# One expert item's rows fetched by a gather, and attention's preparation issued one part earlier, in a one-core decoder layer

## The chip, the core and the metric

The kernel runs on one core of a Trainium2 chip. A core has TensorE (PE, with its weight loads PEld), VectorE (DVE), ScalarE (ACT), GpSimd (POOL) and SyncE (SP), which issues transfers; they run their own instruction lists and meet at semaphores. The metric is the device time of one execution in microseconds.

## What is computed

One layer of a hybrid decoder for 512 prompt tokens and 8 x 8 sample tokens (576 rows of 1024) that share all weights, in float32. In short, from the reference:

```
u -> one projection w_in -> q_lora, kv_lora, k_rope, z, xBC, dt, gate_a, gate_b
branch A: causal conv, chunked SSD scan, gate, RMS norm -> w_branch_a
branch B: latent attention (8 heads; prompt causal, samples over 4096 cached rows) -> w_branch_b
h = LayerNorm(a*u + (sig(gate_a)*y_a + sig(gate_b)*y_b) @ w_out)
logits = h @ router_w + router_b; the top 4 of 32 experts, softmax over the 4
each expert block: rows h[row_tok], SwiGLU with clamps, scaled by the row's gate, added to y
y = LayerNorm(a*h + y)
```

The latent rows, the rotated keys and the scan's states are outputs too.

## The kernel before, in words

`program` runs a row of blocks: latents, prompt attention, sample attention, merge of branch B, convolution, scan, merge of branch A, `stage_choose` (routing), `stage_experts_combine` (experts and last norm). Each block has an instruction list per engine, written out by hand, and ends in a barrier of all engines. Most float32 operands of matmuls are split into a high and a low part (`fp32r`), and three products are summed. A plain float32 product counts as two matmul instructions in the trace, a transpose or an `fp32r` product as one.

**Prompt attention** (`stage_prompt_attention`, lines 368 to 622). 32 steps, i = 4h + q: head h, query block q of 128 rows, against keys 0 to 128(q+1). PE's step i is: the five score products of step i (lines 485 to 489), the transposes of step i-2's probabilities (496), the value products of step i-3 (505), and one of four parts of the preparation of head h+1: part 0 makes the head's query (447), part 1 its key (451), part 2 transposes its rotated query (456), part 3 the samples' query (459). ACT copies each part out with rounding (`prep_copy`, 518 to 527), and DVE forms the remainders of parts 0 to 2 (`prep_rest`, 582 to 587). Buffers of a head are used in pairs (h % 2). PE's scores of a head wait for all three remainders: `prep_low >= 3*h + 3`. Per step, ACT copies step i-2's turned probabilities, takes the exponential of step i (553) and then does `prep_copy`; DVE masks and reduces the scores of step i (600 to 606), normalises step i-1 (611, 613), does `prep_rest`, and copies step i-3's output (622). Before the loop the four parts of head 0 are done. SP stores the samples' queries when all 32 parts are copied, and the next block's gathers of cached rows are issued by POOL.

**Routing** (`stage_choose`, from line 1864). After the output projection and its norm, whose rows `h` stay in SBUF and are stored by SP to `h_rows` in memory (L1931), DVE picks each token's four experts. `rank` is a token's place within an expert, `sel` whether it is chosen. `spot(e)` builds the one-hot tile of expert e's first 128 rows (L2156), for the first three experts. PE then turns `h` into the transposed rows of expert 0 by 40 products with that tile (L2019, in `banks[:, 0:2]`), with the small products on counts and overflow lists between them at k = 2 and k = 6 (L2025, 2026, 2032), and after them makes, by 15 products (L2039), the lists `tok` of row and gate for the three experts. ACT and DVE split the transposed rows into `x_hi` and `x_lo` (L2106, L2248). DVE's list meanwhile computes gates, slots and places (L2214 to L2245). The items after the first get their rows otherwise: POOL gathers them from `h_rows` in the expert loop (L2382), and PE turns them by transposes (L2428).

**Expert loop.** 12 slots of weights per expert, 1 MB each, stream in through SP; the first four of expert 0 are loaded and split ahead, in the routing block. Three products each on PE (L2434).

## Time and profile before

| | |
|---|---|
| three timed runs | 2561.97, 2577.34, 2577.81 us; median 2577.34 |
| profiled execution | 2567.88 us, its span 2566.1 us |
| PE busy | 2350.1 us, 92% of the span |
| DVE, ACT, POOL busy | 1848.2, 1318.4, 461.1 us |
| granted clock of TensorE, mean | 0.951 of full speed |
| attention loop | from 105.63 (first scores) to 210.8 us |
| routing block's tail | from 1336.05 (one-hot products) to 1360.82 us |
| first expert's first product | 1362.56 us |

Times in the trace are microseconds from the span's start. In a time line a row is: start, duration, engine, line, operation, out<-in, shape, count, and in brackets how long the engine was idle before it and who released it; rows of one kind are merged. In a table by stretch a row is: stretch, its length, then for PE, PEld, DVE, ACT and POOL the busy time and in brackets the instructions, then the granted clock as a share of 2.4 GHz, the DMA engines' share and GB/s. A DMA's landing is counted from its issue. Matmuls overlap: the next one starts before the row of the last one ends.

### The profile page before, as it was taken

What the parts mean: (1) busy time and instruction counts of PE and PEld (TensorE: products, weight loads), DVE (VectorE), ACT (ScalarE), POOL (GpSimd) and SP (SyncE); (2) the same over time, 40 slices, a digit from 0 to 9 for tenths busy, and PEclk for the clock granted to TensorE, in tenths of its full rate; (3) what the DMA queues carried; (4) which work ended last, traced back from release to release, by engine and by line L of the source; (5) the groups of instructions that cost most, each with busy time, mean ns of one, the idle gap of its engine ahead of it and who ended that gap; (6) DMA issues with size and microseconds to landing.
All of it is one profiled execution on the core that took longest, in us unless ns stands there. A gap on an engine that the chain in (4) does not pass through costs nothing. (4 is left out here: it accounts for less than half of the span.)

```text
span 2566.1 us, 38723 instructions
## 1 busy us (share of the span) xinstructions
PE 2350.1 (92%) x14479; PEld 1888.2 (74%) x14479; DVE 1848.2 (72%) x2269; ACT 1318.4 (51%) x1412; POOL 461.1 (18%) x403
## 2 busy tenths in 40 slices
PE   8888999989968898699888999999999999999993
PEld 4475566989944444399767888888888888888882
DVE  2565556237756776534556899999999999999997
ACT  1342214223325544431324777777777777777774
POOL 0002220000013333200115222112221222112221
PEclk9998998989979999799978999999999999999997
DMA  5105553322231443222627999999999999999994
GB/s 164 63 1 184 206 198 105 90 72 83 67 125 53 129 134 96 68 78 83 211 88 220 393 395 389 395 382 376 379 379 387 383 374 372 387 383 381 378 372 170
DMA packets 248625, 589.82 MB, mean 230 GB/s; under 512 B 28928, under 2 KB 120320, under 8 KB 244032
## 3 DMA queue, kind: packets, MB, share of 16 engines
q1 hardware_dynamic: 231480, 512.62, 54.5%
q0 software_dynamic: 17024, 75.53, 9.6%
q8 instruction: 84, 1.38, 0.2%
q14 instruction: 37, 0.30, 0.0%
HBM read 551.77 MB, written 36.32 MB: 229 GB/s over the span
## 5 line engine op out<-in xcount | busy, mean ns | idle before, releaser
L2541 DVE TENSOR_TENSOR w_lo<-w_raw,w_hi 128x2048 fp32r<-128x2048 f32 x291 | 660.1, 2289 | 57.9 <-ACT w_hi L2491 56.3
L2491 ACT ACTIVATE w_hi<-w_raw 128x2048 fp32r<-128x2048 f32 x288 | 550.4, 1916 | 134.1 <-PE banks L2434 107.5
L2434 PE MATMUL banks<-w_hi,x_hi 128*128 128x512 f32 x1024 | 319.8, 393 | 2.1 <-DVEq L2580 2.1
L2434 PE MATMUL banks<-w_lo,x_hi 128*128 128x512 f32 x1024 | 316.9, 391 | 0.0
L2434 PE MATMUL banks<-w_hi,x_lo 128*128 128x512 f32 x1024 | 316.3, 390 | 0.0
L2541 DVE TENSOR_TENSOR w_lo<-mergedT,w_hi 128x2048 fp32r<-128x2048 f32 x96 | 220.1, 2293 | 37.3 <-ACT w_hi L2491 37.2
L2434 PEld LDWEIGHTS banks<-w_hi,x_lo 128*128 128x128 f32 x1024 | 192.8, 188 | 41.0
L2434 PEld LDWEIGHTS banks<-w_lo,x_hi 128*128 128x128 f32 x1024 | 192.8, 188 | 40.9
L2434 PEld LDWEIGHTS banks<-w_hi,x_hi 128*128 128x128 f32 x1024 | 190.6, 189 | 39.8 <-DVEq L2580 2.1
L2394 POOL DMA_INDIRECT y_sum<-xT,to_row x32 | 50.9, 1591 | 854.9 <-ACT xT L2523 854.9
L2491 ACT ACTIVATE w_hi<-mergedT 128x2048 fp32r<-128x2048 f32 x96 | 183.8, 1915 | 33.4 <-PE banks L2434 30.5
L2434 PE MATMUL banks<-w_hi,h_hi 128*128 128x512 f32 x512 | 159.0, 392 | 0.6 <-DVE h_lo L2545 0.5
L2434 PE MATMUL banks<-w_hi,h_lo 128*128 128x512 f32 x512 | 158.3, 390 | 0.0
L2434 PE MATMUL banks<-w_lo,h_hi 128*128 128x512 f32 x512 | 158.2, 390 | 0.0
L754 PE MATMUL banks<-keyT,q 32*64 32x256 f32 x2560 | 119.0, 427 | 13.4 <-issue 11.1
L1538 PE MATMUL banks<-wz,xT 128*128 128x512 f32 x256 | 120.0, 624 | 1.2 <-ACT zs L1675 1.2
L754 PEld LDWEIGHTS banks<-keyT,q 32*64 32x64 f32 x2560 | 78.3, 148 | 48.0 <-issue 42.6
L2434 PEld LDWEIGHTS banks<-w_hi,h_hi 128*128 128x128 f32 x512 | 96.4, 189 | 22.0 <-issue 0.9
L2434 PEld LDWEIGHTS banks<-w_lo,h_hi 128*128 128x128 f32 x512 | 96.4, 188 | 20.9
L2434 PEld LDWEIGHTS banks<-w_hi,h_lo 128*128 128x128 f32 x512 | 96.4, 188 | 20.2
L1105 PE MATMUL banks_a<-part_hi_a,w_mhi_a 128*128 128x288 f32 x384 | 83.2, 299 | 17.2 <-DVE w_mlo_a L1141 17.2
L805 ACT ACTIVATE prob<-banks,neg 128x1024 f32<-128x1024 f32 x16 | 17.8, 1115 | 153.0 <-DVE neg L853 153.0
(484 smaller groups left out, 4544.4 us busy)
## 6 DMA issues: line engine op xcount, KB each, us to landing
w_raw<-in_exp_w_gu SPq DMA_DIRECT2D x196, 1024.0 KB
w_raw<-in_exp_w_down SPq DMA_DIRECT2D x96, 1024.0 KB, 9.9
mergedT<-in_exp_w_gu SPq DMA_DIRECT2D x64, 1024.0 KB
mergedT<-in_exp_w_down SPq DMA_DIRECT2D x32, 1024.0 KB, 10.0
w_x<-in_w_in SPq DMA_DIRECT2D x11, 1024.0 KB
out<-h SPq DMA_DIRECT2D x20, 512.0 KB, 2.6
wz<-in_w_in SPq DMA_DIRECT2D x4, 2048.0 KB
dec<-acs_rows SPq DMA_DIRECT2D x16, 512.0 KB, 3.9
```

The source lines that it names most:

```text
L754: mm = pe.matmul(banks[64 * c:64 * (c + 1), i, 0:HALF], q4[at, b % 2, j, :], keyT[at, j, c * HALF:(c + 1) * HALF], start=(j == 0), stop=(j ...
L805: act.activation(prob[:, n % 2].rearrange("p (k i x) -> p i k x", k=BLK, i=4), scores_at.rearrange("p i (k x) -> p i k x", k=BLK), ACT.Exp ...
L1105: mm = pe.matmul(bank_of(u)[:, piece], wp[:, u % NW, k, :], part[:, piece * H2:(piece + 1) * H2], start=(k == 0 and wp is w_hi and n == 0) ...
L1538: mm = pe.matmul(banks[0:n, 7, :], sb.xT[:, q, P * i:P * i + n], wz[:, g % 2, q, :], start=(q == 0), stop=(q == KD - 1))
L2394: pool.indirect_dma_start(out=io.y_sum, out_offset=bass.IndirectOffsetOnAxis(ap=to_row[:, par, :].bitcast(U32), axis=0), in_=y_out, in_off ...
L2434: mm = pe.matmul(banks[:, bank + c, :], x[:, k, :], part[:, s % NHI, j, c * 512:(c + 1) * 512], start=start, stop=last)
L2491: act.activation(w_hi[:, s % NHI], raw(s, par), ACT.Copy).then_inc(hi_ready, 1)
L2541: dve.tensor_tensor(w_lo[:, s % NHI], raw(s, par), w_hi[:, s % NHI].bitcast(F32), ALU.subtract).then_inc(lo_ready, 1)
```

## The change

In attention every part of the preparation is issued as part i+5 in step i, where it was part i+4; five parts stand ahead of the loop. In routing the 40 one-hot products are dropped. Five products with `spot(0)` give, per row of the first item, its token minus T minus its place in the item; DVE adds both back and turns this into an integer row index; POOL gathers the 128 rows from `h_rows` into `x_first`, and PE turns them by 8 transposes, behind the told products. The small products of k = 2 and k = 6 keep their order.

```diff
--- before.py
+++ after.py
@@ -470,8 +470,8 @@
                     mm.then_inc(val_ready, 1)
 
                 pe.wait_ge(rot_out, NT)
-                for part in range(4):
-                    prep(0, part)
+                for m in range(5):
+                    prep(*step(m))
                 pe.wait_ge(val_out, 8)
                 for i in range(n_steps + 3):
                     if i < n_steps:
@@ -504,8 +504,8 @@
                         for k in range(q + 1):
                             mm = pe.matmul(banks[:, 5, 0:P], val[:, k, h, :], probT[:, j % 2, k, :], start=(k == 0), stop=(k == q))
                         mm.then_inc(pv_ready, 1)
-                    if i < n_steps and step(i)[0] + 1 < HEADS:
-                        prep(step(i)[0] + 1, step(i)[1])
+                    if i + 5 < n_steps:
+                        prep(*step(i + 5))
 
             @block.scalar
             def _(act):
@@ -533,8 +533,8 @@
                     i, half = divmod(u, 2)
                     act.wait_ge(val_ready, u + 1)
                     act.activation(val[:, i, 4 * half:4 * half + 4, :], banks[:, 2 + u % 4, :].rearrange("p (h v) -> p h v", h=4), ACT.Copy).then_inc(val_out, 1)
-                for part in range(4):
-                    prep_copy(0, part)
+                for m in range(5):
+                    prep_copy(*step(m))
                 for i in range(n_steps + 2):
                     if i >= 2:
                         j = i - 2
@@ -552,8 +552,8 @@
                             act.wait_ge(pt_ready, i - 1)
                         act.activation(prob[:, i % 2, 0:n], banks[:, 2 + i % 2, 0:n], ACT.Exp, bias=neg[:, i % 2:i % 2 + 1],
                                        scale=ATT_SCALE, accum_out=den[:, i % 2:i % 2 + 1]).then_inc(expd, 1)
-                        if h + 1 < HEADS:
-                            prep_copy(h + 1, q)
+                        if i + 5 < n_steps:
+                            prep_copy(*step(i + 5))
 
             @block.vector
             def _(dve):
@@ -590,8 +590,8 @@
                 dve.wait_ge(kr_high, 2)
                 for a in range(2):
                     dve.tensor_tensor(kr_lo[a * ROPE:(a + 1) * ROPE], sb.krT[:, 0:SEQ], kr_hi[0:ROPE].bitcast(F32), ALU.subtract).then_inc(kr_low, 1)
-                for part in range(3):
-                    prep_rest(0, part)
+                for m in (0, 1, 2, 4):
+                    prep_rest(*step(m))
                 for i in range(n_steps + 3):
                     if i < n_steps:
                         q = step(i)[1]
@@ -611,10 +611,8 @@
                         dve.reciprocal(den[:, j % 2:j % 2 + 1], den[:, j % 2:j % 2 + 1]).then_inc(vec, 1)
                         dve.wait_ge(vec, min(2 * j + 4, 2 * n_steps) + j + 1)
                         dve.tensor_scalar(prob[:, j % 2, 0:n], prob[:, j % 2, 0:n], den[:, j % 2:j % 2 + 1], None, ALU.mult).then_inc(normed, 1)
-                    if 1 <= i <= n_steps:
-                        h, q = step(i - 1)
-                        if h + 1 < HEADS and q < 3:
-                            prep_rest(h + 1, q)
+                    if i >= 1 and i + 4 < n_steps and step(i + 4)[1] < 3:
+                        prep_rest(*step(i + 4))
                     if 3 <= i:
                         j = i - 3
                         h, q = step(j)
@@ -1885,6 +1883,10 @@
         zero = buf("zero", [P, ZW])[:]
         flag, pos, over, before = buf("flag", [E, 4]), buf("pos", [E, 4]), buf("over", [E, 2]), buf("before", [E, 2])
         found = room[0:E, 3 * D + 1280:3 * D + 1280 + 4 * (NOVF + 1)].rearrange("p (j q) -> p j q", j=4)
+        x_first = room[:, 0:D]
+        token_of, first_f = buf("token_of", [P, NT, 2]), buf("first_f", [P, 1])
+        first_row = buf("first_row", [P, 1], I32)
+        first_told, first_put, x_got = sem("first_told"), sem("first_put"), sem("x_got")
         stats, mv = buf("stats7", [P, 2, 6]), buf("mv7", [P, NT, 2])
         banks = ctx.enter_context(nc.psum_tensor("banks7", [P, 8, 512], F32))
         w_in_, first_in = [sem(f"w_in{q}") for q in range(4)], [sem(f"first_in{s}") for s in range(AHEAD)]
@@ -1951,6 +1953,12 @@
                 pool.wait_ge(b_high, 1)
                 pool.tensor_tensor(sb.b_all[E:2 * E], b_raw[E:2 * E], sb.b_all[E:2 * E].bitcast(F32), ALU.subtract).then_inc(b_low, 1)
                 pool.wait_ge(b_low, 2)
+                pool.wait_ge(stored, 16 * NT)
+                pool.wait_ge(cleared, 16 * 3)
+                pool.wait_ge(first_put, 1)
+                pool.indirect_dma_start(out=x_first, out_offset=None, in_=io.h_rows,
+                                        in_offset=bass.IndirectOffsetOnAxis(ap=first_row[:].bitcast(U32), axis=0)).then_inc(x_got, 16)
+                pool.wait_ge(x_got, 16)
 
             @block.tensor
             def _(pe):
@@ -2013,13 +2021,11 @@
                 mm.then_inc(counted, 1)
 
                 pe.wait_ge(spotted, 1)
-                for k in range(KD):
-                    for i in range(NT):
-                        n = ROWS[i]
-                        mm = pe.matmul(banks[:, k // 4, (k % 4) * P:(k % 4 + 1) * P], h[0:n, i, k * P:(k + 1) * P], spots[0:n, 0, i, :],
-                                       start=(i == 0), stop=(i == NT - 1))
-                    if k % 4 == 3:
-                        mm.then_inc(x_ready, 1)
+                for i in range(NT):
+                    n = ROWS[i]
+                    mm = pe.matmul(banks[:, 2, 8:10], spots[0:n, 0, i, :], token_of[0:n, i, :], start=(i == 0), stop=(i == NT - 1))
+                mm.then_inc(first_told, 1)
+                for k in (2, 6):
                     if k == 2:
                         pe.wait_ge(flagged, 2)
                         pe.matmul(banks[0:E, 3, 8:10], K[0:E, K_STRICT:K_STRICT + E], over[:], start=True, stop=True)
@@ -2033,11 +2039,17 @@
                         mm2.then_inc(listed, 1)
                 pe.wait_ge(spotted, LISTED)
                 pe.wait_ge(valued, 1)
+                pe.wait_ge(first_put, 1)
                 for e in range(LISTED):
                     for i in range(NT):
                         n = ROWS[i]
                         mm = pe.matmul(banks[:, 2, 2 * e:2 * e + 2], spots[0:n, e, i, :], vals[0:n, i, e, :], start=(i == 0), stop=(i == NT - 1))
                 mm.then_inc(told, 1)
+                pe.wait_ge(x_got, 16)
+                for k in range(KD):
+                    mm = pe.transpose(banks[:, k // 4, (k % 4) * P:(k % 4 + 1) * P], x_first[:, k * P:(k + 1) * P], K[:, K_ID:K_ID + P])
+                    if k % 4 == 3:
+                        mm.then_inc(x_ready, 1)
 
             @block.scalar
             def _(act):
@@ -2202,12 +2214,17 @@
                 dve.wait_ge(ranked, 1)
                 dve.tensor_copy(rank[:, 0:NT - 1, :], banks[:, 7, 0:4 * E].rearrange("p (i e) -> p i e", i=4))
                 then(dve.tensor_copy(rank[0:NS, NT - 1, :], banks[0:NS, 7, 4 * E:5 * E]))
+                dve.tensor_tensor(token_of[:], K[:, K_VAL:K_VAL + NT].unsqueeze(2).broadcast_to((P, NT, 2)),
+                                  rank[:, :, 0:1].broadcast_to((P, NT, 2)), ALU.subtract)
                 spot(0)
 
                 dve.wait_ge(counted, 1)
                 then(dve.tensor_scalar(flag[:], K[0:E, K_OVER:K_OVER + 4], banks[0:E, 3, 0:1], None, ALU.is_lt))
                 dve.reduce_sum(over[:, 0:1], flag[:], AX).then_inc(flagged, 1)
                 dve.reduce_sum(over[:, 1:2], flag[:], AX).then_inc(flagged, 1)
+                dve.wait_ge(first_told, 1)
+                then(dve.tensor_scalar(first_f[:], banks[:, 2, 8:9], K[:, K_PAIR:K_PAIR + 1], float(T), ALU.add, ALU.add))
+                dve.tensor_copy(first_row[:], first_f[:]).then_inc(first_put, 1)
                 for e in range(1, LISTED):
                     spot(e)
                 dve.wait_ge(based, 1)
```

## Rows read from the trace of the kernel before

**Rows 1.** Waits, 105 to 212 us: line <- releaser: us in total, times, longest.
```profile
PE banks L485 <- DVE qr_two L587: 12.0, 7, 1.7
```

**Rows 2.** Table by stretch, attention: us, then PE, PEld, DVE, ACT, POOL, clock, DMA.
```profile
131.60:144.95 13.35, 11.64 (x73) 9.54 (x72) 8.46 (x30) 6.32 (x20) 0.00 (x0) 1.00 0.01 2
171.60:186.50 14.90, 13.19 (x78) 10.93 (x77) 8.86 (x31) 6.53 (x20) 0.00 (x0) 0.93 0.00 1
```

**Rows 3.** Time line of PE at a head boundary: start, us, line, [idle before <-releaser].
```profile
140.67 0.38 PE L496 MATMUL banks<-const,prob 128*128 128x128 f32 x2
...
141.11 0.56 PE L459 MATMUL banks<-q_new,wkT 128*128 128x64 f32 x4
143.38 0.33 PE L485 MATMUL banks<-k_hi,q_hi 128*128 128x128 f32 x1 [1.71 <-DVE qr_two L587]
...
144.79 2.11 PE L447 MATMUL banks<-qnT,wq 128*128 128x288 f32 x8
146.51 0.49 PE L485 MATMUL banks<-k_hi,q_hi 128*128 128x256 f32 x1
```

**Rows 4.** Time line of DVE at the same head boundary.
```profile
140.87 0.30 DVE L600 TENSOR_TENSOR banks<-banks,const 128x128 f32<-128x128 f32 x1 [0.65 <-PE banks L489]
...
142.19 0.42 DVE L613 TENSOR_SCALAR prob<-prob,den 128x384 f32<-128x384 f32 x1
142.64 0.68 DVE L587 TENSOR_TENSOR qr_two<-banks,qr_two 64x512 fp32r<-64x512 f32 x1
```

**Rows 5.** Time lines of ACT, SP and POOL around the attention loop.
```profile
105.74 1.28 ACT L553 ACT_TABLE_LOAD   x1
...
203.48 0.97 SPq L409 DMA_DIRECT2D q_rows<-qrS  x2
...
212.62 0.94 POOL L362 DMA_INDIRECT rows<-in_cache_kv_latent,page_rows  x1 [134.73 <-POOLq L146]
```

**Rows 6.** Time line of PE: first transposes of the program, then the routing block.
```profile
6.91 1.94 PE L241 MATMUL banks<-const,x_tok 128*128 128x128 f32 x8 [6.91 <-DMA x_tok<-in_x_prompt]
...
1336.05 8.25 PE L2019 MATMUL banks<-w_raw,h 128*128 128x128 f32 x30 [1.26 <-DVE w_raw L2156]
...
1355.51 4.98 PE L2039 MATMUL banks<-vals,w_raw 128*128 128x2 f32 x30
```

**Rows 7.** Time line of DVE in the routing block.
```profile
1336.30 2.64 DVE L2156 TENSOR_SCALAR w_raw<-const,mergedT 128x128 f32<-128x128 f32 x10
...
1344.58 0.15 DVE L2214 COPY before<-banks 32x2 f32<-32x2 f32 x1 [5.64 <-PE banks L2026]
...
1346.74 0.16 DVE L2229 COPY vals<-mergedT 128x15 f32<-128x15 f32 x1
...
1351.77 0.18 DVE L2241 COPY pair<-gate_f 128x20 f32<-128x20 f32 x1
...
1356.24 0.69 DVE L2248 TENSOR_TENSOR x_lo<-banks,x_hi 128x512 fp32r<-128x512 f32 x1 [1.20 <-ACT x_hi L2106]
...
1360.67 0.15 DVE L2252 COPY tok<-banks 128x3 f32<-128x3 f32 x1
```

**Rows 8.** Table by stretch, routing block and expert loop, columns as in rows 2.
```profile
1336.00:1338.00 2.00, 1.95 (x8) 1.78 (x8) 1.97 (x10) 0.00 (x0) 0.00 (x0) 0.50 0.00 0
1358.00:1360.00 2.00, 2.00 (x11) 1.97 (x10) 0.00 (x0) 0.00 (x0) 0.00 (x0) 0.50 0.00 0
1368.00:1370.00 2.00, 2.00 (x10) 1.59 (x9) 1.08 (x1) 0.00 (x0) 1.83 (x2) 0.94 0.88 264
```

**Rows 9.** Told products (L2039) from 1358.5 on: ns min/median/max, starts.
```profile
L2039 PE MATMUL banks<-vals,w_raw x9: 351/353/372, 1358.3 to 1360.1; 128*128 128x2 f32 x7, 64*128 64x2 f32 x2
```

**Rows 10.** POOL gathers (L2382): idle before them until, us, times; landing.
```profile
  POOL from_row L2378: 27.9, 31
...
DMA to landing us min/median/max: 8.6/9.0/10.1
```

**Rows 11.** POOL scatters of the expert loop (L2410): ns min/median/max.
```profile
L2410 POOL DMA_INDIRECT slots<-pair,slot x20: 900/978/2667, 1369.4 to 1404.3; - x20
```

## The prediction

> **What bounds the kernel now.** I read the waits first, then the time lines of the two changed stretches, then the tables by stretch for the clock. The kernel is a row of blocks, and a block's engines start together: when the attention block ends, POOL's first transfer of the next one goes out at once after 134.73 us of idleness, although it needed nothing of attention [rows 5]. So time saved at the end of a block is saved at the end of the program, unless the next block starts differently.
>
> In the attention block PE is the bound: of a head's 13.35 us it is busy for 11.64, DVE for 8.46, ACT for 6.32 [rows 2]. The rest is one wait per head, seven in all and 12.0 us together, always for DVE's remainder of the rotated query, `qr_two` [rows 1]. The time lines show why. Behind the scores of step q = 3 PE comes to two transposes at 140.67, then a value product and preparation part 3, and has nothing from 141.67 until 143.38 [rows 3]. DVE meanwhile masks, reduces and normalises, 140.87 to 142.61, and only then forms the remainder, to 143.32 [rows 4]. The next head's scores need it.
>
> In the routing block two lists stand one behind the other on PE: 40 products of `h` with the one-hot tile, which the trace counts as 80 matmul instructions, two for each fp32 product, from 1336.05; then the 15 products (30 instructions) that tell tokens and gates, 1355.51 to 1360.49 [rows 6]. DVE's last operation on `tok` ends at 1360.82 [rows 7] and the first expert follows behind the block's barrier. The values for the told products were ready at 1346.90 [rows 7], 8.6 us before PE took them up.
>
> **The change, attention.** Nothing is added but order: part i+5 instead of i+4 in step i, one part more ahead of the loop. The remainder of part 2 falls in DVE's round of q = 2, a step before it is needed, so the wait of rows 1 goes: 12.0 us. What is late next: DVE's round from scores to normalised probabilities takes 1.74 us (140.87 to 142.61), and PE now has before its next transposes 0.44 of transposes and values, part 0 (1.72, 144.79 to 146.51) and some 0.6 of scores, five matmuls like that of 143.38 [rows 3]: 2.8 us. Part 0's copies on ACT must be out before part 1; there I count a margin of about 0.5 us, the thinnest. Part 0 itself needs the previous remainder, some 2.2 us after the scores of q = 2, and comes some 3.2 after. So each head should take PE's own 11.64.
>
> Two subtractions. Ahead of the last head there is no part 0 to fill: PE's transposes wait for DVE's 1.74 + 0.09, with only 0.44 + 0.6 of work before them, so 0.8 to 0.9 of the seventh wait comes back here. At the start, part 0 of head 1 goes ahead of step 0, and part 1 must wait for its copies; ACT's table load of 1.28 us, which now stands behind them [rows 5], still ends before the first scores are masked and reduced. Bounds 0 and 1.5; I take 0.4, since copies of about 1.0 have 0.6 of scores beside them. The ten stores of the query rows by SP were issued by 204.45, some 6 us before the block's end [rows 5]; they move earlier by more than the end does and stay covered. Sum: 12.0 - 0.9 - 0.4 = **10.7 us**.
>
> One cycle of the seven took 14.90 us, at a mean granted clock of 0.93 of 2.4 GHz, after the same idle 1.7 us as the others [rows 2]. Gone, it gives 1.5 us more; met twice, it takes 1.5. I count 0.
>
> **The change, routing.** Off PE: the 40 products. On PE: 5 products (10 instructions) that name the first item's token rows, later 8 transposes. On DVE: one small tile ahead of `spot(0)` (0.15 us, the size of L2229 [rows 7]) and two small operations between `spot(0)` and the other spots. On POOL: a wait and one gather of 512 KB; behind it POOL has only the block's end. No DMA of SP moves, and none is under way here; its stores of `h_rows` belong to the rows' norm, long before.
>
> The granted clock is 0.50 here, 1.2 GHz, and I let it stay so with little work on PE [rows 8]. At that level the told instructions start 1.8/8 = 0.22 us apart [rows 9] (I use 0.213, from their unrounded starts), and a list has a tail of 0.14. Step by step:
> - `spot(0)` is done just before PE's 1336.05 [rows 6], 0.15 later now: 1336.2. Ten instructions take 2.27, to 1338.45.
> - DVE's two operations: 0.22 + 0.15 and gaps; `first_put` at 1338.9. They hold the other spots, 2.64 us [rows 7], back to 1341.55.
> - PE has done the two base products. DVE's row from `before` to the gates, 1344.58 to 1346.90 [rows 7], is 2.32 us: values ready at 1343.9.
> - The told products: 30 x 0.213 + 0.14 = 6.5 us, to 1350.4.
> - 8 transposes: nearest row 1.94 us for eight of this shape [rows 6], to 1352.2 with the overlap.
> - ACT's high part with its gaps 0.73 (from 1355.51, when the products end [rows 6], to 1356.24), DVE's low part 0.69 [rows 7], the two `tok` operations 0.37: the block's work ends at 1354.0 instead of 1360.82.
>
> The gather lies beside this. POOL idles 27.9/31 = 0.9 us between index and issue, and the expert loop's gathers, of as many rows, land 9.0 us after issue, 8.6 to 10.1 [rows 10]: 1338.9 + 0.9 + 9.0 = 1348.8, at most 1349.9, before the told products end. It costs nothing because they cover it; without that cover it would cost some 5 us, from 1343.9 to 1348.8. DVE's remaining list, 5.1 us behind the values [rows 7], ends at 1349.35 and hides there too. Gain: **6.8 us**. Upper bound: with the told products at the full clock (3.4 us, to 1347.3) the gather ends last, and the gain is 8.4. Lower: the first rival.
>
> There is a price for POOL beside a busy DVE: its small scatters take 0.98 us typically and up to 2.67 [rows 11]. One such stretch, + 1.7, lands the gather at 1350.5, and the gain is 6.7. The Trainium skill, page "SBUF — State Buffer", section "Who interferes with whom", says more: a DVE operation in a two-port mode, which `tensor_scalar` can enter, and GpSimd take the shared ports exclusively, and the other fully blocks, descriptor generation included. No row here shows a gather beside the spots. By that rule the generation would wait for the spots, which end 1.75 us after its issue, and the sum would be the same within 0.2; by its hardest reading it is the first rival.
>
> What the expert loop finds: before, PE entered it at the low level and was back at the high one soon after 1368 [rows 8], some 6 us in. Now it enters from a longer low stretch; I take the same, with 2.5 us to either side for the range.
>
> **Sum.** 10.7 + 6.8 = 17.5 against the profiled execution's own 2567.88 (its span is 2566.1): 2550.4. That execution and the three timings have a mean of 2571.3; it lies 3.4 below that and 9.5 below the median shown. With 3.4 added: **2554**.
>
> **Rivals.**
> 1. The gather ends last (12%). If POOL builds its descriptors only when DVE's list ends at 1349.35, it lands at 1358.35; transposes, splits and `tok` bring the end to 1361.95, routing loses 1.1: 2571.3 - 10.7 + 1.1 = 2561.7. For it: the scatters' 2.67. Against: 0.98 is the scatters' median, all of them beside a busy DVE.
> 2. Attention's wait moves (12%). If the margin of part 1 is gone and half of each wait returns, for ACT's copies, attention gains 5.4: 2571.3 - 5.4 - 6.8 = 2559.1. For it: the copies stand behind an exponential of the widest step. Against: ACT is busy 6.3 of 13.35.
> 3. Slower (3%). The gather waits where nothing covers it, ahead of the transposes, with the whole block behind it. From a landing time of some 28 us on it has eaten both gains; at 45 us the kernel takes 2571.3 + 17 = 2588. For it: POOL had issued no transfer for hundreds of us. Against: after 134.73 idle us its first one took 0.94 [rows 5], and no gather of this shape landed later than 10.1.
> 4. That the edit does nothing in attention is excluded by the order: DVE's remainder is written one round earlier, and nothing that it reads is later.
>
> **Numbers.** Forecast 73%, own range 2543 to 2564: attention 9 to 12.2, routing 5 to 8.4, and half the 16 us that the four executions of one kernel span. The range 2540 to 2568 takes in the two milder rivals. What a measurement of this kernel can tell from no change is about 1%; against the median shown that bound is 2551.6, against the mean 2545.6. The forecast lies on the near side of both: faster 0.31, within 1% 0.66, slower 0.03.
>
> **What would show it.** Right: no wait of L485 for `qr_two` inside the loop; head cycles of 11.6 to 11.8; the told products start near 1343.9 less attention's gain, the transposes right behind the last of them, and the gather landed before. Wrong: PE idle before the transposes with the gather as releaser, PE idle before part 1 with ACT as releaser, told instructions 0.11 us apart (a high clock), or an expert loop that stays at 1.2 GHz for over 8 us.

## The result, and the profile after

The changed kernel takes **2556.37 us** (median of five, 2549.33 to 2557.95), the kernel before 2575.62 (median of five, 2561.97 to 2577.81): ratio 0.9928, 95% interval 0.9901 to 0.9956. The medians lie 19.3 us apart and the ratio stands for 18.5, near the 17.5 of the sum. The profiled execution took 2556.37 us, its span 2554.6.

To see where the time came from I cut both traces, in the main at the first PE instruction of each block (the scan at its first product with `wz`). Attention: from its first product of part 0 (99.45 before, 101.22 after) to the next block's first product (211.99, 201.18). The routing tail: from DVE's copy of the ranks (1334.21, 1328.21) to the first expert product (1362.56, 1350.26).

| us | before | after | change |
|---|---|---|---|
| attention | 112.54 | 99.96 | -12.6 |
| routing tail | 28.35 | 22.05 | -6.3 |
| latents, ahead of attention | | | +1.8 |
| sample attention | 224.1 | 226.2 | +2.1 |
| scan | 331.1 | 333.6 | +2.5 |
| experts, from the first product on | 1177.0 | 1177.9 | +0.9 |

The two changed blocks give 18.9 us. These two profiled executions differ by 11.5 only, since four blocks happened to be longer in the second one. The other kernels tell whether the change did that. A second profile of the same code has its scan in 330.4 us, and over kernels with identical code there the scan takes 330.3 to 338.7. Sample attention takes 218.6 to 227.8 us in the new order of attention and 224.2 to 226.6 in the old, or, in one set of runs, 174.3 to 175.7 and 176.6. So no effect of the change on these blocks is seen beside their scatter, and the medians agree with the blocks.

**Attention.** PE's waits of the whole block, in the profile of after (line waited at, releaser, total, times, longest):

```profile
PE banks L496 <- DVE prob L613: 2.1, 2, 1.4
...
PE banks L459 <- DVE k_lo L585: 1.0, 2, 0.7
PE banks L505 <- DVE oT L620: 0.5, 1, 0.5
PE banks L451 <- ACT q_new L520: 0.4, 1, 0.4
PE banks L447 <- DVE qr_two L587: 0.3, 1, 0.3
```

The 12.0 us of [rows 1] are gone; the one wait for `qr_two` left is at the start. PE's time line at a head boundary of after, the place of [rows 3]:

```profile
139.99 0.38 PE L496 MATMUL banks<-const,prob 128*128 128x128 f32 x2
140.31 0.46 PE L505 MATMUL banks<-probT,mergedT 128*128 128x128 f32 x2
140.60 2.11 PE L447 MATMUL banks<-qnT,wq 128*128 128x288 f32 x8
142.33 0.44 PE L485 MATMUL banks<-k_hi,q_hi 128*128 128x128 f32 x1
```

Part 0 now stands where the idle 1.71 us stood, and the next head's scores follow at once. The table by stretch, over the same part as [rows 2]:

```profile
127.00:139.00 12.00, 12.00 (x76) 9.91 (x75) 8.80 (x31) 6.72 (x20) 0.00 (x0) 1.00 0.01 2
...
175.00:187.00 12.00, 12.00 (x76) 9.91 (x75) 8.83 (x30) 6.70 (x20) 0.00 (x0) 1.00 0.02 4
```

PE is busy for all of every stretch of the head cycles, and the granted clock stays at 1.00: the slow cycle of [rows 2] has no successor. In the last head the transposes wait 0.71 us for DVE, as foreseen:

```profile
188.29 0.55 PE L496 MATMUL banks<-const,prob 128*128 128x128 f32 x3 [0.71 <-DVE prob L613]
```

**Routing.** PE's time line of after, in the place of the last two of [rows 6]; the kernel's lines are 2026 (names), 2046 (told products), 2050 (transposes), 2451 (first expert):

```profile
1330.13 2.38 PE L2026 MATMUL banks<-token_of,w_raw 128*128 128x2 f32 x10 [1.34 <-DVE w_raw L2168]
...
1336.16 0.64 PE L2038 MATMUL banks<-xT,const 32*1 32x18 f32 x16 [3.40 <-DVE xT L2236]
1337.88 6.98 PE L2046 MATMUL banks<-vals,w_raw 128*128 128x2 f32 x30 [1.08 <-issue]
1344.80 1.97 PE L2050 MATMUL banks<-const,xT 128*128 128x128 f32 x8
1350.26 1.22 PE L2451 MATMUL banks<-w_hi,x_hi 128*128 128x512 f32 x2 [3.49 <-DVEq L2597]
```

The told products start as soon as their values are there, and the transposes follow them with no wait for the gather. The told products take 6.98 us where they took 4.98 before [rows 6]: there the clock stood at 1.00 from 1351.2 to 1358.0 us, behind some 15 us of busy PE, and the first 20 of the 30 instructions started 0.11 to 0.18 us apart. So the change gives up a fast stretch as well as the 40 products. POOL's gather and DVE's spots beside it:

```profile
1333.77 1.16 POOL L1959 DMA_INDIRECT xT<-h_rows,first_row  x1 [48.60 <-DVE first_row L2227]
```

```profile
1332.89 2.66 DVE L2168 TENSOR_SCALAR w_raw<-const,mergedT 128x128 f32<-128x128 f32 x10
...
1337.62 0.16 DVE L2246 COPY vals<-mergedT 128x15 f32<-128x15 f32 x1
...
1348.17 0.15 DVE L2269 COPY tok<-banks 128x3 f32<-128x3 f32 x1
```

How long the gather takes to land, from the second profile of the same kernel, us from issue:

```profile
DMA to landing us min/median/max: 4.5/4.5/4.5
```

The clock of after in the tail, as in [rows 8]:

```profile
1338.00:1345.00 7.00, 7.00 (x31) 6.90 (x32) 4.85 (x12) 0.00 (x0) 0.00 (x0) 0.50 0.00 0
...
1354.00:1356.00 2.00, 2.00 (x8) 1.56 (x7) 2.00 (x2) 0.00 (x0) 2.00 (x2) 0.64 0.99 272
1356.00:1358.00 2.00, 2.00 (x10) 1.66 (x9) 0.99 (x1) 0.00 (x0) 1.84 (x2) 1.00 0.98 332
```

It stays at 1.2 GHz until 1355.4, 5.2 us into the first expert; before it was 5.7.

### The profile page after: what moved, and what is told of

The parts are those of the page before. It is cut to its first block and busy times, and to the rows that moved or that the text cites. A ratio compares the mean times of both kernels' runs of the same rounds, so it can differ in the third digit from the quotient of the medians.

```text
span 2554.6 us, 38605 instructions
## 1 busy us (share of the span) xinstructions
PE 2339.0 (92%) x14417; PEld 1879.6 (74%) x14417; DVE 1847.7 (72%) x2272; ACT 1319.3 (52%) x1412; POOL 469.8 (18%) x404
## 3 DMA queue, kind: packets, MB, share of 16 engines
q8 instruction: 83, 1.36, 0.2%
## 5 line engine op out<-in xcount | busy, mean ns | idle before, releaser
L752 PE MATMUL banks<-keyT,q 32*64 32x256 f32 x2560 | 114.7, 416 | 17.7 <-issue 15.7
L752 PEld LDWEIGHTS banks<-keyT,q 32*64 32x64 f32 x2560 | 76.5, 145 | 50.4 <-issue 44.8
L2451 PEld LDWEIGHTS banks<-w_hi,h_hi 128*128 128x128 f32 x512 | 96.6, 189 | 20.8
```

The lines of the kernel that those rows point to most:

```text
L752: mm = pe.matmul(banks[64 * c:64 * (c + 1), i, 0:HALF], q4[at, b % 2, j, :], keyT[at, j, c * HALF:(c + 1) * HALF], start=(j == 0), stop=(j ...
L2451: mm = pe.matmul(banks[:, bank + c, :], x[:, k, :], part[:, s % NHI, j, c * 512:(c + 1) * 512], start=start, stop=last)
```

## The experiments

Twelve more runs were made in three sets, each on another chip and beside its own runs of the kernel before: `att_only`, `rout_only`, `after_again` and `warm` (before: median 2520.85 us), `early_warm`, `dup_before`, `dup_after` and `gather5` (2568.85), and `kept_warm`, `dup_before_fill`, `dup_before_again` and `early` (2574.45). Ratios are to those, and times of different sets aren't compared by themselves; blocks are cut as above. The `dup_` kernels, `gather5` and `early` were run once each.

### Each part alone, and the whole again

`att_only` has the changed attention and the old routing, `rout_only` the reverse, `after_again` is the changed kernel.

```diff
 # att_only: prompt attention as changed
-                 part i+4 in step i, four parts ahead of the loop
+                 part i+5 in step i, five parts ahead of the loop
 # rout_only: stage_choose as changed
-                 40 one-hot products for the first item
+                 5 naming products, one gather, 8 transposes
```

> Only the attention part of the change. My theory: attention's gain is the seven waits and needs nothing of the routing edit. From PE's first score to the block's end the profile of before has 105.2 us (105.63 to 210.83), of after 90.8 (109.24 to 200.0), with part 0 of 1.8 us moved ahead; from the first part-0 product of head 0 to the next block's first PE product 112.5 and 100.0. I expect 100.0 +- 0.4 here, head cycles of 11.6, and a time about 12 us below before (ratio 0.995); the routing block as before, 28.3 us from DVE's copy of the ranks to the first expert. Rival: a part of those 12 us comes back in the blocks that follow (sample attention took 2.1 us longer in after's profile, the scan 2.5). If that is an effect of the edit, it shows here too, and the ratio is nearer 0.997.

> Only the routing part. My theory: from DVE's copy of the ranks to the first expert's first product 22.0 us as in after (before: 28.35), so about 6.3 us less, ratio 0.9975; attention as before with its seven waits. This is the second sight of attention in its old order: if one cycle of seven again lies at the low clock, that belongs to the idle time of the old order. Sample attention and scan as in before if the 2.1 and 2.5 us of after's profile come from the attention edit; scattered by as much either way if they are only differences between executions.

> The changed kernel once more, for a second profile and more timings. My theory: ratio 0.993 as in the first measurement; attention 100.0 us, routing 22.0, told products start 9.7 us after DVE's copy of the ranks; block lengths of sample attention and scan differ from after's first profile by 1 to 2 us although the program is the same. Rival: they repeat within 0.3 us, and the 4.6 us that after's profile lost in these two blocks is an effect of the change.

| | median us | ratio, 95% | attention | routing tail |
|---|---|---|---|---|
| att_only | 2506.70 | 0.9948 (0.9930 to 0.9966) | 99.9 | 28.4 |
| rout_only | 2513.62 | 0.9971 (0.9951 to 0.9990) | 112.2 | 22.0 |
| after_again | 2500.08 | 0.9917 (0.9890 to 0.9944) | 100.1 | 22.0 |

The parts gain 14.2 and 7.2 us by the medians, together 21.4, and the whole 20.8: they add within the intervals, and in the blocks neither disturbs the other. One expectation for `after_again` missed by far: its sample attention takes 175.7 us and not 1 or 2 off the 226.2 of after (the last section comes back to it). The waits of `rout_only` are those of before again, as its row shows:

```profile
PE banks L485 <- DVE qr_two L587: 12.0, 7, 1.7
```

Its clock also falls once, elsewhere (table by stretch of `rout_only`):

```profile
196.00:209.00 13.00, 10.74 (x68) 9.88 (x68) 8.36 (x30) 5.16 (x15) 0.00 (x0) 0.87 0.24 52
```

Both profiles of the old order have one such stretch (before from 170.2 us on, `rout_only` from 196.7). The changed order, in the eight profiles that keep its attention block as it is, shows 1.00 in every head cycle and 0.97 or more in the last stretch. The next experiments ask whether that is chance.

### How much slack attention has, and what its idle time does to the clock

`dup_before` and `dup_after` do the reduction of each step's scores twice on DVE, in the old and the new order; the extra result is unused.

```diff
+                        dve.reduce_max(mx_again[:, i % 2:i % 2 + 1], banks[:, 2 + i % 2, 0:(q + 1) * P], AX)
                         dve.reduce_max(mx[:, i % 2:i % 2 + 1], banks[:, 2 + i % 2, 0:(q + 1) * P], AX).then_inc(vec, 1)
```

> The kernel before, with each step's maximum taken twice by DVE (the first result is not used): 0.29 to 0.69 us more of DVE in each of 32 rounds, 15.7 us in all. My theory: in the old order DVE's round of q = 3 stands on the path, so each of the seven waits for qr_two grows by the 0.69 us of the widest maximum, from 1.7 to 2.4; with the first and last steps the block from the first part 0 to the next block grows from 112.3 by 5 to 8. Rival: PE was not really held by DVE's round but by something else at the head's change, and the wait stays at 1.7.

> The changed kernel with the same doubled maximum. My theory: in the new order every round of DVE has 2.8 us or more of PE work beside it and takes 1.74 at the widest step, 2.43 with the second maximum, so nothing comes back inside the loop; only the last head's boundary (0.69) and the tail without preparation pay: the stretch grows from 100.0 by 2 to 3.5, head cycles stay at 11.6. Rival: the margins are thinner than I counted, a wait for DVE or ACT appears in every head, and the stretch grows by as much as in the kernel before (5 to 8).

`dup_before` took 2589.41 us, attention 133.2: 20.7 more than before, where 5 to 8 were expected. The wait itself grew as expected (2.3 us each), but the waits explain only about four. They are, in its profile:

```profile
PE banks L486 <- DVE qr_two L588: 15.9, 7, 2.3
PE banks L497 <- DVE prob L615: 1.8, 1, 1.8
```

The rest is in its table by stretch, in the clock:

```profile
118.00:135.00 17.00, 14.71 (x83) 12.18 (x83) 11.40 (x38) 7.16 (x22) 0.00 (x0) 0.91 0.00 0
...
165.00:180.00 15.00, 12.72 (x63) 9.91 (x63) 8.77 (x27) 5.53 (x18) 0.00 (x0) 0.84 0.01 2
180.00:203.00 23.00, 20.75 (x91) 16.79 (x91) 11.74 (x39) 7.08 (x22) 0.00 (x0) 0.72 0.00 1
```

PE idles 2.3 us per head there instead of 1.7, and the clock falls again and again; from 203 us to the block's end at 232 it is 0.79. Neither theory had this, so I ran the same kernel again, and once with that idle time filled by ten matmuls whose result nothing reads:

```diff
 # dup_before_fill, after part 3 of a head
+                            pe.wait_ge(prep_out, 4 * (step(i)[0] + 1) + 3)
+                            for _ in range(10):
+                                pe.matmul(banks[:, 1, :], kr_hi[:, 0:P], kr_hi[:, 0:SEQ], start=True, stop=True)
```

> The kernel before with the doubled maximum, a second look: does the low clock return? My theory: yes, several heads at a mean clock under 0.9, the stretch over 125 us. Rival: the first look was a chance of that execution, and this one is at 117 to 120.

> The kernel before with the doubled maximum, and ten dense products (results unused, 2.2 us at 2.4 GHz) on PE in the place of each head's idle time. With the doubled maximum alone that stretch took 133.2 us instead of 112.3: 21 more, of which the longer waits explain 4 to 8, and the granted clock was 0.76 over four of the heads. My theory: the rest is the clock, lowered because PE stood idle 2.3 us in each head. Then with the idle time filled the clock stays at 1.00 and the stretch is 117 to 121 us. Rival: the loss comes from DVE's longer list itself or from the placement, and the stretch stays at 130 or more.

The second run took 2580.54 us, attention 123.8. Over 125 and several heads under 0.9 were expected, 117 to 120 by the rival: neither came. The waits are the same 15.9, 7, 2.3, and the clock is 0.90 from 118 to 135 us but 1.00 from 135 to 180. The filled kernel took 2579.26, attention 118.3. First the second run, then the filled one, over the same stretch:

```profile
180.00:203.00 23.00, 20.24 (x111) 15.85 (x109) 15.84 (x51) 9.79 (x29) 0.00 (x0) 0.93 0.00 1
```

```profile
180.00:203.00 23.00, 23.00 (x133) 18.32 (x132) 17.09 (x52) 10.31 (x31) 0.00 (x0) 1.00 0.01 1
```

With the hole filled the clock is 1.00 up to 212.4 us, past the last head's start, and only the block's last 6.4 us are at 1.2 GHz; the unfilled runs too end at 1.2 GHz, for their last 5.2 and 5.4 us. The 118.3 lie in the 117 to 121 expected, and DVE's doubled work, the rival, is in the filled kernel too. The filled block is 14.9 and 5.5 us shorter than the unfilled ones. The 5.5 compares two runs of one set; the 14.9 compares two sets, so part of it may be the chip. The fillers bring no result. They stand in the place of PE's idle time, behind one added wait for ACT's copies, and nothing else in the kernel is shorter by them, so what they gain is the clock. So short idle times of PE, once per head, cost clock beyond themselves: 5.5 us within one set. How much differs between two runs of one program (133.2 and 123.8), which were also on two chips, and with one run of each kernel its usual size is not known. The Trainium skill, page "TensorE: Matmul & The Clock Gate", section "A second HAM failure mode: psum-queue depth-cycling", tells of frequent short idle times between groups of matmuls that make the clock swing; these three kernels agree.

`dup_after` took 2548.72 us, attention 108.0: 8.1 more, where 2 to 3.5 were expected. That is a miss. Its waits say what is late next:

```profile
PE banks L497 <- DVE prob L615: 2.9, 2, 1.7
PE banks L506 <- DVE oT L622: 2.9, 7, 0.5
```

No scores wait for `qr_two`. Instead value products wait 0.40 us per head for DVE to have copied out an earlier output. Against after these waits add 0.8 and 2.4 us. The clock takes the larger part of the rest: it is 0.87 from 187 to 203 us, which costs some 2.1, and stays at 1.2 GHz from 202.4 to the block's end at 208.6, so that the last two groups of value products take 1.49 and 2.04 us where after's take 0.88 and 1.13, another 1.5. That leaves 1.3 us which I can't assign. DVE is busy 12.29 of 15 us here, and a head takes 12.0 us, still below the 13.35 of before.

### How long the gather takes, and what it hides behind

`gather5` issues the gather five times, each after the landing of the one before, and PE waits for the last.

```diff
-                pool.indirect_dma_start(out=x_first, ...).then_inc(x_got, 16)
-                pool.wait_ge(x_got, 16)
+                for g in range(5):
+                    pool.indirect_dma_start(out=x_first, ...).then_inc(x_got, 16)
+                    pool.wait_ge(x_got, 16 * (g + 1))
```

> The changed kernel with the first item's gather made five times, one after another's landing, the same rows each time. My theory: in this stretch no other transfer runs and one gather lands 4.5 us after issue, so one has some 6.5 us of cover by the told products; five take 24 to 25 us, to 13 us past the told products' end, and the stretch from the ranks to the first expert is 35 instead of 22.0. Rival (the prediction's row): a gather lands 9 us after issue, five take 45, and the stretch is 55.

It took 2563.69 us, its routing tail 34.3. POOL's time line, then PE's:

```profile
1330.79 1.16 POOL L1960 DMA_INDIRECT xT<-h_rows,first_row  x1 [48.64 <-DVE first_row L2228]
...
1349.76 0.94 POOL L1960 DMA_INDIRECT xT<-h_rows,first_row  x1 [3.62 <-DMA xT<-h_rows,first_row]
```

```profile
1334.90 6.98 PE L2047 MATMUL banks<-vals,w_raw 128*128 128x2 f32 x30 [1.08 <-issue]
1354.04 1.97 PE L2051 MATMUL banks<-const,xT 128*128 128x128 f32 x8 [12.16 <-DMA xT<-h_rows,first_row]
```

Four repeats take 19.0 us and PE waits 12.2, so one gather has some 6.8 us of cover. The tail grows by the 12.2 and nothing else. Expected were 35 for the tail and 6.5 of cover.

### Transposes ahead of the told products, and a clock kept up

With 6.8 us of slack the order on PE could be better: `early` puts the eight transposes ahead of the told products, so that ACT and DVE split the rows beside them. `warm` keeps the old order and puts 63 matmuls into PE's idle time of the routing block, into banks where nothing reads the results; `early_warm` does both, and `kept_warm` adds nine more between the told products.

```diff
 # early
+                pe.wait_ge(x_got, 16)
+                ... 8 transposes of x_first
                 pe.wait_ge(spotted, LISTED)
                 pe.wait_ge(valued, 1)
                 ... told products
-                ... 8 transposes of x_first
 # warm: 20 ahead of turn(NT - 1), 18 after its logits, 4, 15 and 6 further on
+                def keep_busy(count, bank):
+                    for _ in range(count):
+                        pe.matmul(banks[:, bank, :], sb.h_hi[:, 0, :], sb.h_hi[:, 0:4, :], start=True, stop=True)
 # kept_warm, in the told products
+                        if i % 2 == 0:
+                            keep_busy(1, 4)
```

> The changed kernel with its eight transposes ahead of the told products, without the filled clock. My theory: the gather has landed when the values are ready, the 2.0 us of transposes move the told products back, and the splits (two of 0.60 and 0.69 with gaps, 1.5 us) are no longer behind PE's last product: the stretch from the ranks to the first expert is 1.0 us shorter than the 22.0 of the change, at most 1.5. Rival: PE waits for the gather for more than 1 us, and the stretch is 22 or longer.

> The changed kernel with idle PE time of the routing block filled with dense fp32r products of 512 columns into an unused bank (20, 18, 4, 15 and 6 of them, results unused), so as to bring the granted clock to 2.4 GHz. My theory: the told products run at 0.233 us apart because the clock is at 1.2 GHz; at 2.4 they start 0.11 apart, 3.4 us instead of 7.0, the transposes 1.0 instead of 2.0, and the first named-rows list 1.3 instead of 2.4: up to 5 us less in the block, and up to 2.6 us in the first expert if the clock holds over the barrier. Rival: the fill does not raise the clock in time, or itself stands in the way of the small lists (at 1.2 GHz a filler takes 0.43 us, 15 of them 6.4), and the block is 2 to 6 us longer.

> The kernel with the filled clock (20, 18, 4, 15 and 6 dense products whose results are unused), and the eight transposes of the first item put ahead of the told products. My theory: the gather lands 4.5 us after its issue, just before the values are ready, so PE can turn the rows first, and ACT and DVE split them beside the told products. From DVE's copy of the ranks to the first expert: before 28.4, after 22.0, filled clock 18.6; here DVE's list (13.8 us) and its two splits (1.3) end last, 17.3 to 17.8. Time 2 to 4 us below the filled clock alone counting the block, ratio to before 0.988 to 0.990. Rival: PE waits for the gather longer than the splits are worth, and the stretch is 19 or more.

> The kernel with the filled clock and the early transposes, and nine more dense products of 512 columns (results unused) spread over the told products, so that the clock is not lowered before the first expert. My theory: the first expert starts at 1.2 GHz in every version so far and spends 5 to 6 us there, worth 2.5 to 2.8 us; with PE densely busy up to the barrier it starts at 2.4 or is back there within 3 us. The nine cost 0.216 each, 1.9 us of PE, of which the told products' own faster pace gives some 1.7 back. From the ranks to the first expert 17.4 to 18.5, the first expert (first product to first bias product) 1 to 2.5 us shorter than the 13.5 of before. Rival: the idle time at the barrier (2.3 us) alone brings the clock down, and the first expert is unchanged.

"Up to the ranks" is the routing block's first part, from its first PE product to DVE's copy of the ranks. The first column is only to be read beside its own set's kernel before.

| | us | ratio, 95% | up to the ranks | routing tail |
|---|---|---|---|---|
| after | 2556.37 | 0.9928 (0.9901 to 0.9956) | 82.4 | 22.05 |
| early | 2553.53 (one) | | 82.4 | 21.0 |
| warm | 2493.18 | 0.9900 (0.9871 to 0.9930) | 80.3 | 18.6 |
| early_warm | 2544.20 | 0.9893 (0.9870 to 0.9917) | 80.3 | 17.5 |
| kept_warm | 2541.96 | **0.9876** (0.9859 to 0.9893) | 80.3 | 18.2 |

`early` gains 1.1 us of tail, as expected: the transposes now wait for the gather, but the wait is short and ACT's work is covered.

```profile
1335.89 1.97 PE L2042 MATMUL banks<-const,xT 128*128 128x128 f32 x8 [1.53 <-DMA xT<-h_rows,first_row]
1337.65 6.85 PE L2051 MATMUL banks<-vals,w_raw 128*128 128x2 f32 x30
```

Issued at 1331.34, the gather let PE go at 1335.89: again 4.5 us.

`warm` shows that the low clock of this block comes from what PE does there: with fillers in its idle times the clock is 1.00 up to the told products, the names take 1.36 us instead of 2.38 and the told products 4.19 instead of 6.98. But the clock doesn't survive the told products themselves. In `early_warm` (time line, then table by stretch):

```profile
1338.98 1.09 PE L2051 MATMUL banks<-const,xT 128*128 128x128 f32 x8
1339.91 5.07 PE L2060 MATMUL banks<-vals,w_raw 128*128 128x2 f32 x30
```

```profile
1340.00:1342.00 2.00, 2.00 (x19) 1.97 (x17) 1.93 (x4) 0.76 (x2) 0.00 (x0) 1.00 0.00 0
1342.00:1344.00 2.00, 2.00 (x11) 1.97 (x10) 1.93 (x7) 0.00 (x0) 0.00 (x0) 0.51 0.00 0
```

PE is busy for all of both stretches, and in the second the clock is 1.2 GHz. `kept_warm` mixes matmuls of 512 columns in between, and the clock stays at 1.00 through the told products, up to 1336.2. It still doesn't reach the first expert:

```profile
1334.00:1337.00 3.00, 3.00 (x17) 2.35 (x16) 1.87 (x8) 0.00 (x0) 0.00 (x0) 0.87 0.00 0
1337.00:1340.00 3.00, 1.31 (x4) 1.10 (x4) 1.25 (x1) 0.00 (x0) 1.36 (x2) 0.50 0.01 3
...
1342.00:1344.00 2.00, 2.00 (x8) 1.61 (x7) 2.00 (x2) 0.00 (x0) 2.00 (x1) 0.74 0.99 242
```

The rival named the idle time at the barrier. It is there, 1.7 us, but the clock had fallen 0.8 us before it began, in the last filler, with PE busy; what brought it down is not shown. The first product comes at 1338.71 and the high clock at 1343.0, 4.3 us in (5.0 in `early_warm`, 5.2 in after). That isn't a gain by the fillers either: `early` and `gather5`, whose clock is low up to the first expert, have it back after 2.9 and 3.3 us. The nine fillers themselves cost 0.7 us of tail. First product to first bias product takes 13.0 us against 13.4 in `early_warm` and 12.4 in `early`: together nothing, where 1 to 2.5 shorter was expected. `early_warm` and `kept_warm` can't be told apart by their ratios. Of the fillers, `warm` shows the gain beside the changed kernel: its median is 6.9 us below that of `after_again`, of the same set, and 5.5 of that are in the routing block. `early_warm` and `kept_warm` were not run beside the changed kernel; their routing blocks are 6.7 and 6.0 us shorter than its.

## Why the prediction was right

**The order in attention.** Foreseen 12.0 gone, 0.9 back at the last head and 0.4 at the start. Measured, from the waits: 12.0 gone, 0.7 back at the last head, 0.7 at the start (L459 from 0.7 to 1.0, L451 from 0.3 to 0.4, L447 0.3 new). The head cycle is 11.6, from 130.73 to 142.33. Rival 2, that the wait moves to ACT's copies, is refuted: part 1 waits once, 0.4 us, at the start. What is late next was named as DVE's normalised probabilities; doubling DVE's reduction showed a nearer one too, DVE's copies of the output (0.40 per head), which the prediction didn't name.

**The mis-sized term.** The slow cycle of [rows 2] was counted as 0, with 1.5 to either side. It was worth 1.5 of gain: 12.0 - 1.4 + 1.5 = 12.1 of the 12.6 measured. The step "gone or met twice, I count 0" took the clock for a thing apart from the wait. Low stretches come with PE's idle time once per head: in the loop every profile of the old order has at least one, and the filled kernel and the eight profiles of the new order have none (`dup_after`, whose waits are back in part, has one, in the last head). So an order that removes this idle time should have been credited with most of the 1.5.

**Routing.** Gain 6.5 us to the block's last operation against 6.8, and 6.3 to the first expert product. With before's times shifted by the 6.00 us between the two copies of the ranks, the steps read:

| step | foreseen | measured |
|---|---|---|
| names | 2.27 us | 2.38 |
| told products start | 1343.9 - 6.0 = 1337.9 | 1337.88 |
| told products | 6.5 us | 6.98 |
| transposes | 1.94 us | 1.97 |
| block's last operation | 1348.0 | 1348.32 |

The start depended on DVE's list and was right to a few hundredths. The told products are 0.5 long: their mean pitch is 0.236 and not the 0.213 that I took from their last nine [rows 9]. In after most start 0.213 apart, but around each list's product of 64 rows the steps are 0.235 and 0.28. A group of 30 should be priced by 30. The reading that the clock is 0.50 in this part [rows 8] held for the two stretches shown; between them, from 1351.2 to 1358.0, it was 1.00. That did no harm, since the sum priced the told products at the low clock, and after has it.

**The gather.** It was foreseen to cost nothing behind the told products, with 1.6 us to spare. It cost nothing with some 6.8 to spare: 4.5 us to land and not 9.0. The rows that I priced it by [rows 10] are of the expert loop, where weights stream in; after's own loop still takes a median of 8.9 there. POOL's issue alone takes 1.0 us longer there (2.16 against 1.16); that the weights' stream makes the rest is likely, but no run tried it by itself. Rival 1 falls because the gather has landed at 1338.3 while DVE's list runs to 1343.05, and rival 3 by the landing time that `gather5` confirms: 28 us would have been needed to lose both gains. The Trainium skill, page "SBUF — State Buffer", section "Who interferes with whom", would let POOL's descriptor generation wait for the spots. The issue at 1333.77 took 1.16 us in the midst of them, 1332.89 to 1335.55, and the landing 4.5, where the last three rounds of `gather5`, with DVE idle, take 0.94 to issue and 4.6 from one to the next. So POOL didn't wait for the spots to end; a wait for a single one of them (0.27 us each) isn't excluded by these rows.

**The clock in the tail** was taken as 0.50 throughout and was; the entry into the expert loop was taken as 6 us low and was 5.2.

**The sum**: 17.5 foreseen, 18.9 in the two blocks, 18.5 by the ratio. The forecast of 2554 lies 2.4 below the median. That these lie so close is in part luck: by its interval the ratio stands for 11 to 26 us, and before's median of five is 4.3 above the mean that the forecast started from. What tests the terms is the two blocks: attention 12.6 for 10.7, with the clock's 1.5, and routing 6.3 for 6.8.

## What to carry to other kernels

Price a small idle time of the bounding engine by its clock too: look whether a low stretch lies among the waits, and credit their removal with it. Price a transfer by rows taken under the load that it will meet: a gather of the same size took half the time on idle queues. And where a list of tiny products has to run, put the work that other engines need ahead of it, as soon as its input has landed (`early`: 1.1 us).

## What the runs showed of the hardware

- With idle times of 2.3 us once per head the mean granted clock over 23 us was 0.72 in one run and 0.93 in another of the same program, on another chip; with the idle times filled it was 1.00.
- The clock fell to 1.2 GHz some 2 us into the told products (`early_warm`, 1342) although PE was busy all the time, with matmuls of two columns; in before it fell at 1358.0, 2.5 us into them, likewise. In `kept_warm`, with a 512-column matmul after every one or two of these products, it stayed at 2.4 GHz through them, 5.6 us, and fell in the last 512-column matmul.
- The first expert starts at 1.2 GHz in every profile, behind 1.7 to 3.5 us of idle PE at the barrier, and is back at 2.4 GHz after 2.9 to 5.7 us. In `kept_warm` the clock had fallen 0.8 us before that idle time.
- A gather of 128 rows of 4 KB landed 4.5 us after its issue with the queues idle, 8.9 (median) beside weights at some 385 GB/s.
- The sample attention block took 219 to 228 us in the later two sets of runs and in the first pair of profiles, and 174 to 177 in all four profiles of the set whose before had a median of 2520.85, with the same code. Nearly all of the 50 us between after and `after_again` is idle time of PE before the products of its scores (L752) with no releaser that the profile shows: 60.5 us in 105 pieces against 10.2 in 20. That set ran on another chip than the later two; whether this is the cause was not tried.
